# A mixture of experts for 256 tokens: gathered expert rows replaced by one stream of all experts, with a dense weight matrix from one-hot products, and the two tiles' mixers meshed

## The reference

```
q      = h @ w_pq                                # 8 heads, two halves of 128
s0, s1 = q[half 0] @ keys0.T, q[half 1] @ keys1.T   # 128 scores each
v0, i0 = top_k(s0, 16); v1, i1 = top_k(s1, 16)
best, at = top_k(v0[:, None] + v1[None, :], 16)  # of 256 candidates
expert = i0[at // 16] * 128 + i1[at % 16]        # 16 per head: 128 per token
weight = softmax(best)
out    = sum over the 128 of weight * gelu(h . expert_u[expert]) * expert_v[expert]
x      = x + gate * out
```

## Time and profile before

| | before |
|---|---|
| time, median of 3 | 1441.12 us (1440.86 to 1446.74) |
| span of the profiled execution | 1423.6 us |
| TensorE busy in it | 1023.0 us (72%) |
| VectorE busy | 921.9 us (65%) |
| ScalarE busy | 357.7 us (25%) |
| moved by DMA | 391.10 MB |

### The profile page before, as it was taken

How to read it: one execution, slowest core, us unless ns; L and a number is a source line. 1 busy time by engine, 2 the same in 40 slices (tenths; PEclk the granted TensorE clock), 3 DMA queues, 4 the chain that set the end, 5 groups by cost and what they waited for, 6 DMA issues and landing times.

```text
span 1423.6 us, 17219 instructions
## 1 busy us (share of the span) xinstructions
PE 1023.0 (72%) x6241; PEld 594.2 (42%) x6241; DVE 921.9 (65%) x2443; ACT 357.7 (25%) x813; POOL 288.0 (20%) x265
## 2 busy tenths in 40 slices
PE   7997999999899999978868668664543354543434
PEld 4776656577665556436534323332211122211111
DVE  5488633448864437544366788778777676777765
ACT  2013523101443412455244532321011110001100
POOL 0000000000000000000033334545433444433441
PEclk9998999999899899999979888976756666665765
DMA  8462562455456242162179899999999999999996
GB/s 295 150 193 98 187 220 89 162 178 165 144 182 222 63 144 96 59 239 90 34 290 412 327 420 418 418 414 419 415 421 415 419 414 416 417 414 414 420 421 274
DMA packets 111926, 391.10 MB, mean 275 GB/s; under 512 B 10971, under 2 KB 39182, under 8 KB 79586
## 3 DMA queue, kind: packets, MB, share of 16 engines
q0 software_dynamic: 37440, 268.45, 45.8%
q1 hardware_dynamic: 74402, 121.56, 24.7%
HBM read 387.89 MB, written 1.05 MB: 273 GB/s over the span
## 4 chain that ended last, share of the span: by engine, by line
DMA 21%; DVE 18%; PE 14%; ACT 4%; POOL 3%; issue 3%; DVEq 0%; ACTq 0%
DMA e_uv<-in_experts_dram,e_listed 21%; PE bank L169 13%; DVE e_uv L2814 5%; POOL e_uv L3021 3%; ACT m_W L229 1%; DVE e_rest L2745 1%; DVE e_diag L185 1%; ACT L229 1%; PE bank L174 1%; DVE e_hot L185 1%; DVE e_si L2743 1%; DVE e_si L2749 1%; DVE e_sv L2747 1%; DVE e_sv L2741 1%; DVE m_W L185 1%
## 5 line engine op out<-in xcount | busy, mean ns | idle before, releaser
L3021 POOL DMA_INDIRECT e_uv<-in_experts_dram,e_listed x252 | 278.9, 1107 | 1098.8 <-DVE e_listed L202 823.0
L169 PE MATMUL bank<-e_uv,e_diag 128*32 128x512 f32 x1024 | 232.1, 884 | 321.6 <-DVE e_diag L185 321.6
L2814 DVE CUSTOM_DVE_ANT_0 e_uv<-e_uv,e_h2q 128x1024 f32<-128x1024 f32 x192 | 229.3, 1221 | 84.5 <-DMA e_uv<-in_experts_dram,e_listed 84.1
L169 PEld LDWEIGHTS bank<-e_uv,e_diag 128*32 128x32 f32 x1024 | 41.5, 139 | 445.9 <-DVE e_diag L185 363.7
L169 PE MATMUL bank<-hT,weights 128*128 128x256 f32 x640 | 145.1, 388 | 2.7 <-DVE hT L191 1.4
L169 PEld LDWEIGHTS bank<-hT,weights 128*128 128x128 f32 x640 | 123.6, 195 | 22.3 <-issue 1.9
L229 ACT ACTIVATE e_act<-e_dot 128x4 f32<-128x4 f32 (+1 forms) x81 | 16.6, 205 | 394.7 <-DVE e_dot L2814 393.9
L229 ACT ACT_TABLE_LOAD x81 | 103.9, 1283 | 10.8 <-DVE e_dot L2814 2.8
L169 PE MATMUL bank<-weights,hT 128*128 128x512 f32 (+1 forms) x256 | 101.5, 552 | 2.2 <-DMA weights<-in_w_in_dram 2.2
L197 DVE SCALAR_TENSOR_TENSOR conv<-ubuf,vec,conv 128x256 f32<-128x256 f32 x240 | 96.8, 480 | 0.6
L2814 DVE CUSTOM_DVE_ANT_0 e_uv<-e_uv,e_hT 128x1024 f32<-128x1024 f32 x64 | 76.3, 1220 | 20.6 <-DMA e_uv<-in_experts_dram,e_listed 20.6
(11 more groups left out here) (384 smaller groups left out, 1414.1 us busy)
## 6 DMA issues: line engine op xcount, KB each, us to landing
weights<-in_w_in_dram SPq DMA_DIRECT2D x16, 2048.0 KB, 8.1
weights<-in_w_ada_dram SPq DMA_DIRECT2D x8, 2048.0 KB, 8.7
weights<-in_w_out_dram SPq DMA_DIRECT2D x6, 2048.0 KB, 7.8
e_w_pq<-in_w_pq_dram SPq DMA_DIRECT2D x12, 1024.0 KB, 26.3
weights<-in_cmp_w_dram SPq DMA_DIRECT2D x4, 2048.0 KB, 8.4
m_w<-in_w_in_dram SPq DMA_DIRECT2D x2, 2048.0 KB, 8.1
m_wo<-in_w_ada_dram SPq DMA_DIRECT2D x2, 2048.0 KB, 8.4
m_w<-in_w_ada_dram SPq DMA_DIRECT2D x2, 2048.0 KB, 10.2
```

The costliest lines, as they stand in the source:

```text
L169: ins = self.engine.matmul(out, lhsT, rhs, start=start, stop=stop, **kw)
L2814: dve.mark(c.nc.vector.tensor_tensor_reduce(u, u, h2q[tt][n], 1.0, 0.0, MUL, ADD, m["dot"][:, j:j + 1]), ("dots_set", g, c0) if n == c1 - ...
L3021: ins = c.nc.gpsimd.indirect_dma_start(out=to, out_offset=None, in_=rows, in_offset=bass.IndirectOffsetOnAxis(ap=of, axis=0))
```

## The change

Nothing is gathered any more. The experts' u and v come in 64 chunks of 256 experts (1 MB each, laid out on the host so that a partition's 8 KB are one piece), once for all 256 tokens. In the first pass TensorE multiplies every chunk of u with all tokens' h2T (`hidden`: 16 products with 256 columns), ScalarE takes GELU of the result out of PSUM, and SP stores it in DRAM (`hidden_dram`, 256 KB a chunk; the last three chunks stay in SBUF). Meanwhile the routing goes on, now with the 8 heads of a tile one after another. When a tile is routed, a dense matrix of weights (every expert, every token) is built: for each token TensorE multiplies a one-hot matrix of the 128 slots' first numbers (`picks_i`) with one of their second numbers times the weight (`picks_j`), four tokens to a bank, and ScalarE copies the 128 x 128 results to `dense` (two tiles of 64 KB per partition). In the second pass the stored values return (`room`), VectorE multiplies them with the dense weights (`weighed`), and TensorE adds v (`summed`: 8 products with 512 columns). `behind_chunk` says which routing and dense work stands behind each chunk. The mixers of the two tiles are meshed head by head ahead of all this, and the first tile's routing stands around the end of the second tile's mixer. The diff, cut to its core:

```diff
+    two.levels(0)
+    one.att_turned(2)
+    one.outputs(2)
+    one.att_values(2)
+    two.lstm_scores(0)
+    two.att_scores(0)
...
+PAIR = 2
+CHUNKS = N_KEYS // PAIR
+RING, STAGES, HEADS_HELD = 4, 3, 4
+GROUP = 4
+GROUPS = P // GROUP
+TURNS = [(h, tt) for tt in range(NT) for h in range(PEER_H)]
+HALF = PEER_H // 2
+KEPT = (CHUNKS - 3, CHUNKS - 2, CHUNKS - 1)
+SUMS = KEPT + tuple(range(CHUNKS - 3))
+ROOMS = STAGES + 4
+def behind_chunk(n):
+    work = [(kind, PEER_H + i) for i in range(PEER_H) for kind, at_chunk in (("q", 2 + 2 * i), ("s", 3 + 2 * i)) if at_chunk == n]
+    work += {13: [("soft", 0)], 17: [("turned", 0)], 28: [("soft", 1), ("picks", 0, 0), ("picks", 0, 1)], 34: [("turned", 1)]}.get(n, [])
+    work += [("dense", 0, g) for g in range(GROUPS) if 29 + g * 19 // GROUPS == n]
+    work += [("dense", 1, g) for g in range(GROUPS) if 48 + g * 15 // GROUPS == n]
+    return work
...
+    def hidden(n):
+        bank = take("u", n)
+        view = ring[:, n % RING].rearrange("p (e k i) -> p e k i", e=PAIR, k=KT)
+        pe.wait_ge(*at(f"ring{n % RING}_in", n))
+        for e in range(PAIR):
+            for kt in range(KT):
+                pe.mm(bank[:, e * T:e * T + T], view[:, e, kt, :], h2T[:, kt, :], start=kt == 0, stop=kt == KT - 1,
+                      tell=filled("u", n) if (e, kt) == (PAIR - 1, KT - 1) else None)
+    def dense(tt, g):
+        bank = take("dense", tt, g)
+        if tt == 0:
+            pe.wait_ge(*at("picks_i_by_act", tt, g))
+        pe.wait_ge(*at("picks_set", tt, g))
+        for i in range(GROUP):
+            pe.mm(bank[:, i * N_KEYS:(i + 1) * N_KEYS], m["picks_i"][:, g % 2, i, :], m["picks_j"][:, g % 2, i, :],
+                  tell=filled("dense", tt, g) if i == GROUP - 1 else None)
+    def summed(n):
+        m_in = CHUNKS + n
+        view = ring[:, m_in % RING].rearrange("p (e d) -> p e d", e=PAIR)
+        room = m["rooms"][room_of(n)]
+        pe.wait_ge(*at(f"ring{m_in % RING}_in", m_in))
+        pe.wait_ge(*at("weighed", n))
+        last = n == CHUNKS - 1
+        work = [(tt, e, h) for tt in range(NT) for e in range(PAIR) for h in range(2)]
+        if last:
+            work.sort(key=lambda w: (w[0], w[2]))
+        for tt, e, h in work:
+            tell = None
+            if last and e == PAIR - 1:
+                tell = ("sum_done", tt, h)
+            elif (tt, e, h) == work[-1]:
+                tell = ("rows_added", n)
+            pe.mm(acc[tt][h][:, :], room[:, e, tt * P:tt * P + P], view[:, e, h * 512:h * 512 + 512],
+                  start=n == 0 and e == 0, stop=last and e == PAIR - 1, skip_group_check=True, tell=tell)
...
+    for n in range(CHUNKS):
+        hidden(n)
+        for kind, *a in behind_chunk(n):
+            if kind == "q":
+                queries(*a)
+            elif kind == "s":
+                scores(*a)
+            elif kind == "turned":
+                turned(*a)
+            elif kind == "dense":
+                dense(*a)
...
+        sp.wait_ge(*c.full("u", n))
+        rows(n + RING)
+        for kind, *a in behind_chunk(n):
+            if kind == "s" and a[0] + HEADS_HELD < len(TURNS):
+                head(a[0] + HEADS_HELD)
+        if n not in KEPT:
+            sp.wait_ge(*c.taken("u", n))
+            sp.load(hidden[n], m["stage"][:, n % STAGES].rearrange("p e t -> p (e t)"), f"stored{n % STAGES}", n)
+    for n in range(len(KEPT), ROOMS):
+        room(n)
+    for n in range(CHUNKS - 1):
+        sp.wait_ge(*at("rows_added", n))
+        if n + RING < CHUNKS:
+            rows(CHUNKS + n + RING)
+        if n + ROOMS < CHUNKS:
+            room(n + ROOMS)
...
+    def picks(tt, g):
+        if tt:
+            shape = [P, GROUP, N_KEYS]
+            dve.tt(m["picks_i"][:, g % 2], wide(K["iota"].unsqueeze(1), shape),
+                   wide(slots[:, 0, g * GROUP:g * GROUP + GROUP].unsqueeze(2), shape), ALU.is_equal, settled=False)
+        for i in range(GROUP):
+            t = g * GROUP + i
+            dve.ts(m["picks_j"][:, g % 2, i, :], K["iota"], slots[:, 1, t:t + 1], ALU.is_equal, slots[:, 2, t:t + 1], MUL,
+                   settled=False, tell=("picks_set", tt, g) if i == GROUP - 1 else None)
+    def weighed(n):
+        of = SUMS[n]
+        if of in KEPT:
+            dve.wait_ge(*c.taken("u", of))
+        else:
+            dve.wait_ge(*at(f"room{room_of(n)}_in", n))
+        if n == 0:
+            dve.wait_ge(*c.taken("dense", 1, GROUPS - 1))
+        dense = m["both_dense"]
+        far = (N_KEYS + RING * PAIR * D // P) * P
+        both = bass.AP(dense.tensor, dense.offset + of * PAIR * P, [dense.ap[0], [far, 2], [P, PAIR], [1, P]])
+        room = m["rooms"][room_of(n)].rearrange("p e (a t) -> p a e t", a=NT)[:, ::-1]
+        dve.tt(room, room, both, MUL, tell=("weighed", n))
...
-    def dots(g, c0, c1):
-        tt = TURNS[g // PER_TURN][1]
-        for n in range(c0, c1):
-            j = PLACE[g] * BATCH + n
-            dve.wait_ge(*at(f"uv_in{j}", g))
-            if n == c0 and BEFORE[g] is not None:
-                dve.wait_ge(*at("gelu_set", *last_part(BEFORE[g])))
-            if g // PER_TURN == FIRST_OF[tt] and n == c0:
-                dve.wait_ge(*c.taken("h2q", tt, QUARTERS - 1, 1))
-            u = m["uv"][j][:, 0:D]
-            dve.mark(c.nc.vector.tensor_tensor_reduce(u, u, h2q[tt][n], 1.0, 0.0, MUL, ADD, m["dot"][:, j:j + 1]),
-                     ("dots_set", g, c0) if n == c1 - 1 else None)
...
+    def hidden(n):
+        act.wait_ge(*c.full("u", n))
+        if n >= STAGES:
+            act.wait_ge(*at(f"stored{n % STAGES}", n - STAGES))
+        act.f(m["stage"][:, n % STAGES].rearrange("p e t -> p (e t)"), c.banks.tile("u", n), ACT.Gelu, tell=c.banks.emptied("u", n))
+    def picks(tt, g):
+        to = m["picks_i"][:, g % 2]
+        for i in range(GROUP):
+            t = g * GROUP + i
+            act.f(to[:, i, :], K["iota"], ACT.Abs, bias=m["slots"][tt][:, 0, t:t + 1], settled=i == 0)
+        act.f(to, to, ACT.Relu, scale=-1.0, bias=K["ones"][:, 0:1], tell=("picks_i_by_act", tt, g))
...
-def peer_gpsimd(c, m, A, x):
-    pool, at = c.pool, c.at
-    halves = A["experts"].rearrange("n (a d) -> (n a) d", a=2)
-    def fetch(to, rows, of, *tell):
-        ins = c.nc.gpsimd.indirect_dma_start(out=to, out_offset=None, in_=rows, in_offset=bass.IndirectOffsetOnAxis(ap=of, axis=0))
-        c.events.tell(ins, *tell, by=16)
```

More of the change, by code:

```diff
@@ L1813, in __init__ @@
         self.c, self.m, self.K, self.tt, self.s = c, m, K, tt, m["tile"][tt]
-        self.values, self.out = c.banks.tiles[(4, 6)[tt]], c.banks.tiles[6:8]
+        self.values, self.out = c.banks.tiles[4], c.banks.tiles[6:8]
     def att_scores(self, *heads):
@@ L2714, in peer_sync @@
-def peer_sync(c, m, mix, A, x, out):
-    sp, at = c.sp, c.at
-    sp.wait_ge(*c.full("rope", len(HEAD_WORK) - 1))
-    for k in range(len(TURNS)):
-        if k == 5:
-            sp.wait_ge(*at("mix_done", 1, 0, 1))
-            mix_load(c, mix, A, "out1 again")
-        if key_turn(k) == k:
-            load_head(c, m, A, k)
+    two.attention_turned()
+    two.mix_out(0)
+    queries(2)
+    scores(1)
+    two.lstm_turned(0)
+    two.lstm_turned(1)
+    two.mix_out(1)
+    for k in range(3, PEER_H):
+        queries(k)
+        scores(k - 1)
@@ new lines, in experts_tensor @@
+    scores(PEER_H - 1)
+    two.normed_turned()
+    pe.wait_ge(*at("x_mixed", 1))
+    pe.wait_ge(*at("att_ready", 1))
+    c.banks.rotate(0, 1, 2, 3, 5, 4, 6, 7)
+    for half in range(2):
+        pe.wait_ge(*c.taken("h2T", 1, half))
+    for n in range(CHUNKS):
[9 more added lines that the diff above has]
+                dense(*a)
@@ new lines, in experts_vector @@
+    halves(1)
+    two.mixed()
+    candidates(1)
+    two.mean_inverse()
+    two.normed()
+    halves(2)
+    two.filled(1)
+    candidates(2)
+    for k in range(3, PEER_H):
+        halves(k)
+        candidates(k)
+        if k == HALF - 1:
+            places(0, 0)
+    places(0, 1)
+    gaps(0)
+    for k in range(PEER_H, 2 * PEER_H):
+        halves(k)
+        candidates(k)
+        if k == PEER_H:
+            soft(0)
+        if k == PEER_H + HALF - 1:
+            places(1, 0)
+    places(1, 1)
@@ L3048, in program @@
-def program(nc, A, out, counted):
+    two.attention_turned()
+    two.lstm_root(0)
+    two.lstm_root(1)
+    queries(2)
+    scores(1)
+    two.lstm_turned(0)
+    two.lstm_turned(1)
+    queries(3)
+    scores(2)
+    two.squares()
+    queries(4)
+    scores(3)
+    two.root()
+    for k in range(5, PEER_H):
+        queries(k)
+        scores(k - 1)
+    scores(PEER_H - 1)
+    two.filled(0)
+    for n in range(CHUNKS):
+        hidden(n)
+        for kind, *a in behind_chunk(n):
+            if kind == "q":
+                queries(*a)
+            elif kind == "s":
+                scores(*a)
+            elif kind == "soft":
+                soft(*a)
+            elif kind == "turned":
+                turned(*a)
+            elif kind == "picks":
```

(5 more changed lines are left out.)

928 lines of the change are left out of this document (372 added, 556 removed).

## The result

The changed kernel takes 1773.16 us in the median of 4 runs (1772.95 to 1778.87), the kernel before, run beside it, 1443.8 us (1440.86 to 1446.74): a ratio of 1.227 (95% interval 1.222 to 1.232). The change makes it slower by 329 us. The forecast was 1782 us in a range of 1755 to 1830.

The account below looks back on a forecast made before the run. TensorE's products were taken to bound the changed kernel: 783 + 442 + 33 + 57 + 1 + 3 + 440 + 5 = 1764 us of span, plus 17.5 us around it, so 1782 us, in a range of 1755 to 1830.

Parts of the forecast that it names:

- What would bound it: Whole changed kernel: TensorE bound throughout at full clock, its products after the mixers costing 973 us; 75 in 100.
- Hidden values, routing, one-hot products and waits inside: First chunk to first sum: 442 us hidden products, 33 second tile's routing, 57 one-hot, 1 turning slots, 3 waits for VectorE.
- Weighted sums: Second expert pass: 512 products of 512 columns at 0.859 us each, 440 us.
- The end: After TensorE's last product: two VectorE steps of 0.69 us and a store, 5 us.
- Mixers up to the first chunk: Both tiles' mixers and the first tile's routing: from 641 us, 121 of work plus 21 idle, first chunk at 783 us.
- The 21 us of waits: TensorE idle in the mixers: about 8 us before the second tile, 10 before normed rows, 3 before the first chunk.
- the mesh: Mixers of both tiles interleaved: first chunk at 783 us, against 786 to some 800 with no overlap.
- From span to run: Step from profiled span to median run time: 17.5 us added, taking 1764 us to 1782.
- Costed at nothing: Stream, ScalarE, VectorE and their picks during the expert passes: assumed covered by TensorE's products, adding no time.
- the rival of 6 in 100: First tile's dense part: ScalarE bounds it if the strided copy makes a group cost 7 us; +75, 1857 us; 6 in 100.
- The DMA share: Sign for the windows of the chunks: near 0.45, with TensorE over 95% busy at clock near 1.00.
- The first rival: Expert chunks: cheap products leave the stream bounding, span 1281, 1299 us in all, deciding from 0.265 us down; 1 in 100.

Follow-up runs that it names:

- e1: Changed kernel with each expert-row transfer after the first four chunks cut to an eighth, products using stale rows: 1773.59 us.
- e5: Changed kernel with ScalarE's GELU of each chunk and copy of each one-hot group issued twice: 1772.52 us (one run).
- e2: Changed kernel with only four of eight row blocks entering the hidden values, 512 products fewer: 1569.87 us (one run).
- e4: Changed kernel with both expert passes multiplying bf16 (rows converted on load, tokens and weighed values rounded), sums in float32: 1300.34 us, ratio 0.910 to the kernel before.
- e3: Changed kernel with the two tiles' mixers run one after the other instead of meshed, the rest as changed: 1770.33 us.
- e6: e4 with each expert-row transfer after the first four chunks cut to an eighth, sums using stale rows: 1211.27 us (one run).
- e10: Changed kernel with bf16 products, serial mixers, six ring slots, first tile's row picks on VectorE, and bf16 GELU values: 1240.77 us, ratio 0.861 to the kernel before.

## Why the prediction was right, and where it was off

- **What would bound it.** Right, and shown from both sides: less stream (e1) and more ScalarE (e5) change nothing, fewer products (e2) or cheaper ones (e4) change it at once.
- **Hidden values, routing, one-hot products and waits inside.** The sum gave 442 + 33 + 57 + 1 + 3 = 536 us; from the first chunk at 793.87 us to the first sum at 1328.47 us it was 534.6. The two waits for picks were 2.0 us against 3.
- **Weighted sums.** 440 us in the sum, 1761.07 + 7.03 - 1328.47 = 439.6 measured. The end took 3.5 us against 5.
- **Mixers up to the first chunk.** 783 us in the sum, 793.87 measured: the step that was mis-sized, by 11 us. The 21 us of waits were right (21.3). The work was set at 121 us from 641; it took 130.3 from 642.27. TensorE's clock is part of that: the three stretches up to 760 us cost up to 13.6 us by it, while the row of before that I scaled from the earlier trace rows had (1 - 0.92) x 60 = 4.8 us in it, and some 4 more when scaled to the second tile. That explains up to 5 of the 9 us. Another 1.6 us are a misreading: in the stretch of before from 640 to 700 us the modulations took about 4.4 us (the rows below, one more of 1.12 us at 659.14, and the end of one before 640.3), where I had taken off 6 for the second tile. The other 3 us and the start's 1.3 stay open. And the mesh, which I valued at 3 to 17 us against the tiles without overlap (786 to 800), was worth nothing (e3): I had walked through the waits that it removes and not through those that it makes.

```profile
646.60 1.92 PE L169 MATMUL bank<-m_w,cond_sT 128*32 128x512 f32 x16
648.45 1.12 PE L169 MATMUL bank<-cond_mod_rows,constants 128*128 128x512 f32 x2
```
- **From span to run.** I added 17.5 us for "what lies around the span". That step was wrong. The profiled execution of the changed kernel took 1772.95 us with a span of 1771.6, and the runs of the kernel before beside the experiments have 1.4 to 1.6 us around their spans. The 17.5 us were a difference between executions of the kernel before: its profiled execution has a span of 1423.6 us, and none of the three runs in the table of before took less than 1440.86. With 1.4 in its place the forecast would have been 1765 us. The span came out 7.6 us above its sum (10.9 for the mixers, less 1.4, 0.4 and 1.5 for the three pieces above), and the 17.5 us covered that: the forecast lies 9 us above the result instead of 8 below. That the two errors have opposite signs is luck, though either alone stays inside the range.
- **Costed at nothing.** The strided copy of the one-hot group took 585 ns, as the copy of the earlier trace rows, so the rival of 6 in 100 had no ground; the picks took 346 ns where the bound was 0.40. Loads of 1 MB landed in about 5 us. ScalarE waited 335.6 us for TensorE, so the cover was wide; but e2 shows that it has its first gaps when a chunk costs half, and in e4, at a quarter, VectorE, ScalarE and the stream each set the time in a stretch. The DMA share was sized at 0.45; it was 0.52 and 0.53 in the two phases, without effect.
- **Rule and row.** The Trainium skill, "FP8 and Floating Point Precision", TensorE Precision Notes, says that true FP32 takes four passes. Measured: 0.431 us for 256 columns in float32 (4.04 cycles a column at 2.4 GHz), and 0.216 us for 512 columns in bf16 (1.01): the trace agrees. The sentence of the Trainium skill, "TensorE: Matmul & The Clock Gate", Step-by-step, on one column per cycle holds here for bf16 alone.
- **The first rival.** It named the stream at 417 GB/s and 1281 us of span as what cheap products would give, with 0.265 us per 256 columns as the point that decides. With products at 0.109 the span was 1296.8 (e4): but only the second phase was then the stream's (e6); the first was bound by VectorE's routing and ScalarE's picks. So half of the rival's mechanism was real, its condition was false in float32, and that its total comes within 16 us of e4's span is in part luck.

## What to carry to other kernels

Before trading gathered bytes for dense products, multiply the number of products by the price of one from a run of the same type in the same trace; the engine that idles half the time may be asked for more than the span. Once the price of a product is cut, the next limits come one behind another (here the routing on VectorE, one-hot passes on ScalarE, the stream), and each is found by the engine that is full in its own stretch. A mesh of two chains can win at most the idle time of the serial order (18.0 us here), and it brings waits of its own at its far end, where no partner is left; walk through both before counting on it (here 21.6 us of idle, so nothing was won).

## What the hardware showed that I had not expected

The kernel bound by transfers differed by more between occasions (medians of 1443.8, 1427.6 and 1438.0 us for the same kernel, single runs from 1426.66 to 1452.32) than the one bound by TensorE: 1773.16 us, and 1773.59 with its stream cut (e1), single runs from 1772.95 to 1778.87. Why is not shown. A copy of 512 columns that reads every 128th value of a bank and writes groups of four values 128 places apart costs ScalarE 585 ns, what the copy of the earlier trace rows does; single values at a stride were not written in any run. Transfers that convert float32 to bf16 keep the pace of plain ones counted by what they read: in e4 1.05 MB of rows and 0.26 MB of values were read for each chunk of about 3.16 us (seven from 1100.56 to 1122.70 us), 414 GB/s, as the gather's 412 to 421 before, though only 247 GB/s by what landed. In e10 1.05 and 0.13 MB in 2.87 us give 411 GB/s.
